# Keys and values of the input projection: from twelve full products to six pairs of seven block products

## The reference, cut to what matters

```
xn = rmsnorm(x, norm_mix)
proj = xn @ w_in                       # 1024 x 5888
q, k, v, cb, cc, ch, ga, gb = split(proj, (768, 768, 768, 512, 512, 512, 1024, 1024))
att, kv_rows = dilated_attention(q, k, v, rel_bias, kv_bufs)   # three head groups, dilation 1, 4, 16
...                                    # gated convolution, gates, x += m @ w_o, MLP, final rmsnorm
```

## Time and profile before

| | |
|---|---|
| median of 3 runs | 1650.33 us (1646.99 to 1653.42) |
| the profiled execution | 1651.21 us, of which its span (first to last instruction) is 1649.4 us |
| PE busy | 1609.4 us, 98% of the span |
| DVE, ACT, POOL busy | 858.1, 568.8, 77.0 us (52%, 34%, 5%) |
| keys and values, steps 6 to 17 | about 103 to 266 us of the span |
| mean granted TensorE clock | 0.995 of 2.4 GHz |

### The profile page before, as it was taken

How to read it: one execution, slowest core, us unless ns; L and a number is a source line. 1 busy time by engine, 2 the same in 40 slices (tenths; PEclk the granted TensorE clock), 3 DMA queues, 4 the chain that set the end, 5 groups by cost and what they waited for, 6 DMA issues and landing times.

```text
span 1649.4 us, 30030 instructions
## 1 busy us (share of the span) xinstructions
PE 1609.4 (98%) x11087; PEld 1556.1 (94%) x11087; DVE 858.1 (52%) x1560; ACT 568.8 (34%) x1057; POOL 77.0 (5%) x101
## 2 busy tenths in 40 slices
PE   8999899999999999999999999999999999999997
PEld 7899898898988999999999999999999999999997
DVE  6112122333645444433656866666666665656686
ACT  5212123433534443211334514333241515152342
POOL 0160000000000000000023000000000000000012
PEclk9999999999999999999999999999999999999999
DMA  5444554322347877542222354453626172635512
GB/s 166 117 138 132 154 164 141 107 93 89 117 111 189 188 181 196 149 129 87 66 91 88 98 176 135 147 163 112 199 85 222 57 233 72 204 103 175 186 42 109
DMA packets 248351, 223.16 MB, mean 135 GB/s; under 512 B 26926, under 2 KB 222342, under 8 KB 248282
## 3 DMA queue, kind: packets, MB, share of 16 engines
q1 hardware_dynamic: 218574, 186.66, 38.2%
q10 hardware_dynamic: 26268, 28.31, 5.1%
q0 software_dynamic: 3440, 7.26, 1.5%
HBM read 153.46 MB, written 71.08 MB: 136 GB/s over the span
## 4 chain that ended last, share of the span: by engine, by line
PE 88%; DVE 4%; issue 2%; ACT 2%; DMA 1%; SPq 1%; ACTq 1%; DVEq 0%; POOL 0%; POOLq 0%
PE bank L764 14%; PE bank L765 13%; PE bank L766 13%; PE bank L1212 7%; PE bank L1213 7%; PE bank L1214 7%; PE bank L1132 6%; PE bank L1131 6%; PE bank L1130 6%; PE bank L885 1%; PE bank L918 1%; PE bank L987 1%; PE bank L904 1%; PE bank L831 1%; PE bank L1037 1%
## 5 line engine op out<-in xcount | busy, mean ns | idle before, releaser
L764 PE MATMUL bank<-xhi,wh 128*128 128x352 f32 (+1 forms) x1104 | 374.0, 339 | 10.5 <-DVE wl L1842 7.4
L765 PE MATMUL bank<-xlo,wh 128*128 128x352 f32 (+1 forms) x1104 | 362.2, 328 | 0.0
L766 PE MATMUL bank<-xhi,wl 128*128 128x352 f32 (+1 forms) x1104 | 361.6, 328 | 0.0
L764 PEld LDWEIGHTS bank<-xhi,wh 128*128 128x128 f32 x1104 | 208.7, 189 | 22.5 <-DVE wl L1842 8.0
L1212 PE MATMUL bank<-fhi,uh 128*128 128x368 f32 (+1 forms) x672 | 219.9, 327 | 0.4 <-DVE flo L2291 0.4
L1213 PE MATMUL bank<-flo,uh 128*128 128x368 f32 (+1 forms) x672 | 220.0, 327 | 0.0
L1214 PE MATMUL bank<-fhi,ul 128*128 128x368 f32 (+1 forms) x672 | 218.9, 326 | 0.0
L765 PEld LDWEIGHTS bank<-xlo,wh 128*128 128x128 f32 x1104 | 208.9, 189 | 0.0
L766 PEld LDWEIGHTS bank<-xhi,wl 128*128 128x128 f32 x1104 | 208.9, 189 | 0.0
L1658 ACT ACTIVATE uh<-uraw 128x512 fp32r<-128x512 f32 x135 | 85.0, 629 | 338.8 <-PE bank L1214 242.2
L1842 DVE TENSOR_TENSOR wl<-wr,wh 128x1024 fp32r<-128x1024 f32 x70 | 86.2, 1232 | 170.2 <-ACT wh L1312 170.2
(11 more groups left out here) (267 smaller groups left out, 2786.8 us busy)
## 6 DMA issues: line engine op xcount, KB each, us to landing
uraw<-in_w_ff_dram SPq DMA_DIRECT2D x128, 256.0 KB, 3.5
xring<-d_x SPq DMA_DIRECT2D x60, 544.0 KB, 4.5
d_x<-xring SPq DMA_DIRECT2D x56, 544.0 KB, 3.1
wr<-in_w_in_dram SPq DMA_DIRECT2D x46, 512.0 KB, 4.3
d_T<-stg ACTq DMA_DIRECT2D x18, 544.0 KB, 3.0
kvc<-in_cache_kv_g_dram SPq DMA_DIRECT2D x16, 512.0 KB, 6.0
...
```

Source lines behind the costliest of these rows:

```text
L764: pe.matmul(bank[c][:, 0:n], wh[st_.p][:, k, :], a, start=(k == 0), stop=False)
L765: pe.matmul(bank[c][:, 0:n], wh[st_.p][:, k, :], b, start=False, stop=False)
L766: last = pe.matmul(bank[c][:, 0:n], wl[st_.p][:, k, :], a, start=False, stop=(k == nk - 1))
```

## The change

Six pairs of tiles take the place of the twelve steps. For pair q the tokens are halved (544 each), the input features are parted into even and odd tiles, and seven units replace the eight block products. Ahead of them, among the q steps 2 to 5, DVE builds the sums and differences of the token and feature halves of x (`x_sums`), and ACT and DVE split them to hi and lo (`x_parts`, `x_lo_parts`) into `txa` and `txb`. Weights come as four blocks of 256 KB into `uraw`. The turning is now done two tiles at a time: `turn_second` (8 transposes) right after unit 6, `turn_first` (10 transposes) after unit 0 of the next pair, or after the first prompt chunk behind the last pair. The stores of both tiles of a pair to token-major places stand together in `turned_act_2`. The loops on ACT and DVE are written out, so the addresses of these stores are constants. Semaphore counts of the later stages are shifted by the 42 units.

```
+KV_PAIRS, KV_UNITS = 6, 42
...
+    txa = at("txa", [P, 2, 2, KF, HALF], RB, F32R)
+    txb = at("txb", [P, 2, 2, KF, HALF], RC, F32R)
+    xraw = [at(f"xraw{i}", [P, 2, TOK], off) for i, off in enumerate((RB + 34816, RB + 53760))]
+    u3x = at("u3x", [P, HALF], RB + 34816)
...
-        with sp.Fori(0, 2) as i:
-            for k in range(6):
-                weights(W_IN[:, :, ds(i * ATT_W + (ATT_W + k * P), P)], KD, Step(6 + k, (6, i)))
+        def kv_load(slot, q, *wait):
+            sp.wait_ge(*wait)
+            sp.dma_start(uraw[slot][:], kv_source(slot, q)).then_inc(r_in[slot], 16)
+        for slot in range(4):
+            kv_load(slot, 0, w_lo, 5 + slot // 2)
+        for q in range(1, KV_PAIRS):
+            kv_load(A11, q, kv_sum, 4 * q - 1)
+            kv_load(A21, q, u_lo, 7 * q - 4)
+            kv_load(A22, q, u_lo, 7 * q - 2)
+            kv_load(A12, q, u_lo, 7 * q)
+        sp.wait_ge(u_lo, KV_UNITS)
+        for p in range(2):
+            sp.dma_start(wr[p][:], W_IN[:, :, prompt_col[0] + p * P:prompt_col[0] + (p + 1) * P]).then_inc(w_raw[p], 16)
...
+        sp.wait_ge(u_done, KV_UNITS)
         pair(0, 0)
-        for p in range(2):
-            unit_weights(0, 0, p)
...
+        def turn(q, m, grp, out):
...
+        def turn_second(q):
+            pe.wait_ge(kv_ev, kv_at(q, 7))
+            for grp in range(2):
+                turn(q, 1, grp, 2 + grp)
+        def turn_first(q):
+            pe.wait_ge(kv_ev, kv_at(q, 10))
+            pe.wait_ge(stg_a, 6 + 2 * (q + 1))
+            for grp in range(3):
+                turn(q, 0, grp, 4 + grp)
+            turn(q, 1, 2, 7)
+        def kv_unit(u, operand, b0, fresh=True):
+            pe.wait_ge(u_lo, u + 1)
+            p = u % 2
+            for c in range(2):
+                out = banks8[:, b0 + c, 0:HT]
+                for k in range(KF):
+                    a, b = operand(0, k, c), operand(1, k, c)
+                    pe.matmul(out, uh[p][:, k, :], a, start=fresh and k == 0, stop=False, skip_group_check=True)
+                    pe.matmul(out, uh[p][:, k, :], b, start=False, stop=False, skip_group_check=True)
+                    last = pe.matmul(out, ul[p][:, k, :], a, start=False, stop=k == KF - 1, skip_group_check=True)
+            last.then_inc(u_done, 1)
...
+        def kv_pair(q):
+            if q == 0:
                 for c in range(3):
-                    pe.wait_ge(taken[c], kv + 7)
-
+                    pe.wait_ge(taken[c], 6)
                 pe.wait_ge(bt_a, 3)
                 pe.wait_ge(const_d, 2)
-
+            else:
+                pe.wait_ge(stg_a, 6 + 2 * q)
+            kv_unit(7 * q, x_block(0, 0), 0)
+            if q:
+                turn_first(q - 1)
+                pe.wait_ge(tm_d, 4 * q - 3)
+                pe.wait_ge(tm_a, 2 * q - 1)
+            else:
+                pe.wait_ge(x_lo, 2 * TILES + 8)
+            kv_unit(7 * q + 1, t_block(txb, 1), 2)
+            if q:
+                pe.wait_ge(tm_d, 4 * q - 2)
+                pe.wait_ge(tm_a, 2 * q)
+            kv_unit(7 * q + 2, t_block(txa, 1), 4)
+            if q:
+                pe.wait_ge(tm_d, 4 * q)
+            kv_unit(7 * q + 3, t_block(txa, 0), 6)
+            pe.wait_ge(kv_ev, kv_at(q, 2))
+            kv_unit(7 * q + 4, t_block(txb, 0), 4, False)
+            pe.wait_ge(kv_first, q + 1)
+            kv_unit(7 * q + 5, x_block(1, 0), 0, False)
+            pe.wait_ge(kv_ev, kv_at(q, 5))
+            kv_unit(7 * q + 6, x_block(1, 1), 6, False)
+            turn_second(q)
...
-        for kv in range(12):
-            for c in range(3):
-                chunk(Step(6 + kv), KD, c, xhi, xlo)
-                if kv:
-                    turn(kv - 1, (kv - 1) % 6, c)
+        for q in range(KV_PAIRS):
+            kv_pair(q)
...
             if first:
+                pe.wait_ge(stg_a, 6 + 2 * KV_PAIRS)
                 chunk(st0, KD, 0, xhi, xlo)
-                for c in range(3):
-                    turn(11, 5, c)
-
+                turn_first(KV_PAIRS - 1)
+                chunk(st0, KD, 1, xhi, xlo)
                 pe.wait_ge(tm_d, 24)
                 pe.wait_ge(tm_a, 12)
                 scores(g, i, 0)
-                chunk(st0, KD, 1, xhi, xlo)
+                chunk(st0, KD, 2, xhi, xlo)
                 scores(g, i, 1)
-                chunk(st0, KD, 2, xhi, xlo)
...
+        def kv_hi(q, i):
+            src, *wait = ((uraw[A11], r_in[A11], 16 * (q + 1)), (s2, kv_sum, q * 4 + 2), (uraw[A21], kv_sum, q * 4 + 3),
+                          (s1, kv_sum, q * 4 + 1), (uraw[A22], r_in[A22], 16 * (q + 1)), (uraw[A12], r_in[A12], 16 * (q + 1)),
+                          (uraw[A12], kv_sum, q * 4 + 4))[i]
+            u = 7 * q + i
+            act.wait_ge(*wait)
+            if u < 2:
+                act.wait_ge(ready, 3 * (5 + u))
+            else:
+                act.wait_ge(u_done, u - 1)
+            act.activation(uh[u % 2][:], src[:], ACT.Copy).then_inc(u_hi, 1)
+        def x_parts(k):
...
+            for m, out in enumerate((txa, txb)):
+                act.activation(out[:, :, 0, k, :], halves(xraw[k % 2][:, m, :]), ACT.Copy).then_inc(x_hi, 1)
...
+        def turned_act(q):
+            token_major(q, 1)
+            kv_store(q, 0)
+        def turned_act_2(q):
+            token_major(q, 0)
+            for m in (1, 0):
+                kv = 2 * q + m
+                token_major_store(kv, kv // 6, kv % 6)
+        def kv_act(q):
+            kv_hi(q, 1)
+            if q:
+                turned_act(q - 1)
+            kv_hi(q, 2)
+            if q:
+                act.wait_ge(kv_ev, kv_at(q, 0))
+            else:
+                act.wait_ge(ready, 18)
+            act.wait_ge(u_done, 7 * q + 1)
+            act.activation(split2(u2[:]), two(0), ACT.Copy).then_inc(kv_first, 1)
+            if q:
+                turned_act_2(q - 1)
+            for i in range(3, 7):
+                kv_hi(q, i)
+            act.wait_ge(stg_st[0], 16 * (3 + q))
+            if q:
+                act.wait_ge(tm_pe, 6 * q)
+            act.wait_ge(u_done, 7 * q + 6)
+            for c in range(2):
+                for out, lo, hi, dil in stage_half(0, q % 3, 0, c):
+                    act.activation(out, undilated(banks8[:, c, lo:hi], dil), ACT.Copy).then_inc(stg_a, 1)
+            if q + 1 < KV_PAIRS:
+                kv_hi(q + 1, 0)
+            else:
+                act.wait_ge(u_done, KV_UNITS - 1)
+                split_hi(Step(S_PROMPT), KD)
+            kv_store(q, 1)
...
+        qkv_step(Step(3), d_T[0], 3, None, 0)
+        x_parts(0)
+        x_parts(1)
+        qkv_step(Step(4), d_T[0], 4, None, 0)
+        x_parts(2)
+        qkv_step(Step(5), d_T[0], 5, None, 0)
+        x_parts(3)
+        for q in range(KV_PAIRS):
+            kv_act(q)
+        turned_act(KV_PAIRS - 1)
+        turned_act_2(KV_PAIRS - 1)
...
+        def turned_dve(q):
+            token_major(q, 0, 0, 3)
+            token_major(q, 0, 2, 5)
+            token_major(q, 1, 2, 6)
+        def kv_lo(q, i):
+            u = 7 * q + i
+            src = (uraw[A11], s2, uraw[A21], s1, uraw[A22], uraw[A12], uraw[A12])[i]
+            dve.wait_ge(u_hi, u + 1)
+            dve.tensor_tensor(ul[u % 2][:], src[:], f32(uh[u % 2][:]), ALU.subtract).then_inc(u_lo, 1)
...
+        def kv_dve(q):
+            kv_lo(q, 1)
+            if q:
+                token_major(q - 1, 1, 0, 1)
+            kv_lo(q, 2)
+            if q:
+                turned_dve(q - 1)
+            dve.wait_ge(kv_first, q + 1)
+            dve.wait_ge(u_done, 7 * q + 2)
+            dve.tensor_tensor(split2(u2[:]), two(2), split2(u2[:]), ALU.add).then_inc(kv_ev, 1)
+            kv_lo(q, 3)
+            dve.wait_ge(u_done, 7 * q + 3)
+            dve.tensor_tensor(split2(u3x[:]), two(4), split2(u2[:]), ALU.add).then_inc(kv_ev, 1)
+            kv_lo(q, 4)
+            dve.wait_ge(kv_ev, kv_at(q, 2))
+            kv_staged(q, 1, 1, 6, u3x, 3, True)
+            kv_lo(q, 5)
+            kv_sum_4(q)
+            kv_staged(q, 1, 0, 4, u2, 4, False)
+            kv_lo(q, 6)
+            if q + 1 < KV_PAIRS:
+                kv_sum_1(q + 1)
+                kv_lo(q + 1, 0)
+                kv_sums_23(q + 1)
+            else:
+                dve.wait_ge(u_lo, KV_UNITS)
+                dve.wait_ge(kv_sum, 4 * KV_PAIRS)
+                split_lo(Step(S_PROMPT), KD)
+            kv_staged(q, 0, 1, 6, u2, 6, True)
+        def x_sums(k):
+            b1, b2 = xraw[k % 2][:, 0, :], xraw[k % 2][:, 1, :]
+            first, second = slice(0, HALF), slice(HALF, TOK)
...
+            for m, b in enumerate((b1, b2)):
+                dve.tensor_tensor(b, f32(xhi[:, 2 * k + m, :]), f32(xlo[:, 2 * k + m, :]), ALU.add).then_inc(x_sum, 1)
+            dve.tensor_tensor(b1[:, first], b1[:, second], b1[:, first], ALU.subtract).then_inc(x_sum, 1)
+            dve.tensor_tensor(b1[:, second], b2[:, second], b1[:, second], ALU.subtract).then_inc(x_sum, 1)
```

(53 more changed lines are left out.)

166 lines of the change are left out of this document (103 added, 63 removed).

## The result

The changed kernel takes 1662.01 us (median of 4 runs, 1661.05 to 1663.05); the kernel before, run beside it, 1650.26. The ratio is 1.0072 with a 95% interval of 1.0051 to 1.0092: slower, by 11.8 us, inside the forecast range of 1640 to 1671 and 5 us above the 1657 forecast. The profiled execution took 1661.05 us (span 1659.3) against 1651.21 (1649.4).

What follows compares the result with a forecast made beforehand. PE, busy 98% of the span, was taken to bound the kernel. Costs of 31.8 us against gains of 25.1 gave +6.7, so a profiled 1657.9 and a median of about 1657 us, range 1640 to 1671.

Steps and rivals of the forecast that it cites:

- the price of a product: In the tile steps and pairs, fewer columns: 12 x 12.85 us becomes 42 x 3.007 plus 108 transposes, gaining 16.1 us.
- the cases: Outcomes for the whole kernel: forecast (waits and lost clock) 0.50, Rival A 0.20, Rival B 0.13, Rival C 0.17.
- Rival B: Before unit 3, ACT issues both store sets within 3.2 us, so its weights come in time: 1632 us; chance 0.13.
- the two sets: A pair's two tiles of stores on ACT ahead of unit 3's weights, between 5.4 and 7.1 us, taken as 6.0.
- Rival C: In each pair the second store set takes 4.5 us behind another, lengthening waits: +8, so 1665 us; chance 0.17.
- Rival A: The waits come but TensorE's clock stays up, so its loss drops out: 1649 us; chance 0.20.
- the entry: Before pair 0's first units, DVE's added work makes PE wait: 3.5 us (2 to 6), plus 1.4 of lost clock.
- gain 2: Between the two loop rounds, written-out ACT and DVE loops remove the 6.52 us wait and 2.5 of slow stretch: 9.0 us.
- unit 0 then covers `x_lo_parts(3)`: At the entry, unit 0's 3.0 us covers `x_lo_parts(3)` and `ul`, 3.2 us, leaving a wait of 0.2.
- the exit: After the last pair, 1.8 us waiting for prompt weights and 3.0 for stores ahead of the table load.
- The ten stores ahead of the table load: At the exit, the last pair's stores on ACT delay table load and exponentials: 3.0 us (1 to 4.5).
- cost 4: Lower clock behind six waits (entry, four, one) loses 8.0 us (0 to 15); a wait of 2.8 loses 1.5.

Runs made afterwards that it cites:

- spread_act: Changed kernel with each pair's stores still on ACT but spread, two or three behind each weight split of units 3 to 6; 1636.98 us, 0.9919 of the kernel before.
- set_per_gap: Changed kernel with stores on ACT, one tile's behind unit 3's weights, the other's behind unit 4's; 1635.08 us, 0.9910 of the kernel before.
- stores_on_sp: Changed kernel with the stores of pairs 0 to 4 issued by SyncE, the last pair's still on ACT; 1633.98 us, 0.9909 of the kernel before.
- exit_on_sp: stores_on_sp with the last pair's stores also on SyncE, behind its loads for the first attention pair; 1629.64 us, 0.9863 of the kernel before.
- before_no_drain: Kernel before with ACT and DVE loops written out and a round's last tile copied and stored among the next step; 1641.31 us, ratio 0.9940.

## Why the forecast was right, and where it was off

**Right: what bounds, and the price of a product.** Pricing by repeats instead of listed durations held to 0.1 us: -16.1 forecast, 6 x (25.70 - 23.03) = -16.0 measured. (A slip that changes nothing: by their shares the cases make faster 0.14 and same 0.49, not 0.15 and 0.48.)

**Right: the wait and its cause.** Stores on ACT ahead of the weights of unit 3 stall TensorE in pairs 1 to 5, longest in pair 3. spread_act, set_per_gap and stores_on_sp take it away in three ways with the transfers unchanged. Rival B (fast issue) was wrong: it needed 3.2 us for two sets, which took 4.9. The Trainium skill ("DMA: Bandwidth & Descriptors", section "Issuing engines are not separate DMA queues") calls the initiating time usually small beside the transfer; for one store the trace agrees in part: in pair 1 of the changed kernel each 512 KB store was issued in 0.40 us and landed 2.5 to 2.8 us later, the 32 KB ones were issued in 0.6 to 0.8 and landed 1.6 to 2.3 later. What decided here is the number of them in one engine's queue: eight issues hold ACT for 4.9 us.

**Mis-sized: the two sets.** Taken at 6.0 us, measured 4.9. The four usual waits were 2.0 to 2.6 us, not 2.8; the ten stores (7.6 against 7.55) and their wait (4.63 against 4.3) were as priced. So 13.6 for 15.5. Rival C, a second set slowed to 4.5 us in every pair, did not come: with four stores it took 2.3 to 2.7 us. The second sets with five stores took 4.3 in pair 3 and 4.8 behind the last pair.

**Right in size: the clock.** 8.3 us behind five waits, and filling them gave it back. The forecast of 8.0 was for six waits, so its closeness is luck in part: the entry's 1.4 did not come. Rival A (the clock stays) is out. The rule of the Trainium skill ("TensorE: Matmul & The Clock Gate", section "HAM oscillation — how this bites in real kernels") that only longer idle gaps take the clock down did not hold: waits of 1.98 to 2.63 us were each followed by the lower level. But mine, 1.5 us for any such wait, was no law either: 2.20 and 1.65 us at the entry cost nothing in the changed kernel, while the lower level followed the same first wait in exit_on_sp.

**Right in size, wrong in its parts: gain 2.** 9.0 forecast, 9.5 measured by before_no_drain. I put it to the loops being written out. What the rows show is the order at the round's end, where the last tile's copy and stores stand ahead of the next split; no run has the one without the other.

**Partly wrong: the entry.** 2.20 us by DVE's queue, as worked out (2.6). The second wait was forecast at 0.2 and was 1.65: the step "unit 0 then covers `x_lo_parts(3)`" left out ACT, which makes the hi parts only after its copy of step 5. DVE stood still for 1.77 us on them:

```profile
106.93 1.29 DVE L2187 TENSOR_TENSOR txa<-xraw,txa 128x1088 fp32r<-128x1088 f32 x1 [1.77 <-ACT txa L1526]
```

**The step that failed: the exit.** 4.8 us forecast, 8.1 left over for it in the account. "The ten stores ahead of the table load: 3.0 (1 to 4.5)" was too low: by exit_on_sp they cost 6.0. Of these 4.0 are idle time, inside my bounds. The other 2.1 are the clock, which I had put at nothing here: cost 4 prices six waits and not this one, which was the longest (5.42 us, and a mean clock of 0.65 in the 8.3 us behind it). The weights of the first prompt steps were forecast at 1.8; a wait of 1.17 us stands there, and the other 0.9 or so of the remainder is not placed.

**Why the total came near all the same.** In the profiles the exit (+3.3) and the low clock near the kernel's end (+3.3), which no step of mine had, stand against the overpriced waits before unit 3 (-1.9) and the gain in the attention (-1.5). Together that is +3.2, and the profiled 9.8 exceed the forecast 6.7 by 3.1. The medians lie 2 us further apart, at 11.8. So part of the nearness of 1657 to 1662 is luck: misses in both directions cancelled.
